# HGRN2 mixer of a 16-block network: work on keys, log decays and the first two levels moved between the weight slabs of its projections

## The reference

```python
q, f, i, g = jnp.split(h @ w_in, ...)                 # four projections, 1024 columns each
log_f = jnp.logaddexp(jnp.log(lb), jnp.log1p(-lb) + jax.nn.log_sigmoid(f))
k = -jnp.expm1(log_f)                                 # = (1 - lb) * sigmoid(-f)
q = jax.nn.silu(q);  v = i
# per head (8 heads of 128), cum = cumsum(log_f) over the tokens:
# o[t] = sum over s <= t of (q[t] * exp(cum[t] - cum[s]) . k[s]) v[s]
o = _rms(o, out_gain) * jax.nn.silu(g)
return o @ w_out
```

## Time and profile before

| | us |
|---|---|
| median of 3 runs | 2720.44 (2717.47 to 2721.78) |
| profiled execution: its own time | 2737.34 |
| profiled execution: span of the trace | 2735.2 |
| PE / DVE / ACT busy in the span | 2615.1 / 1762.1 / 1313.4 |
| PE / DVE / ACT share of the chain that ended last | 91% / 3% / 2% |

### The profile page before, as it was taken

How to read it: one execution, slowest core, us unless ns; L and a number is a source line. 1 busy time by engine, 2 the same in 40 slices (tenths; PEclk the granted TensorE clock), 3 DMA queues, 4 the chain that set the end, 5 groups by cost and what they waited for, 6 DMA issues and landing times.

```text
span 2735.2 us, 60697 instructions
## 1 busy us (share of the span) xinstructions
PE 2615.1 (96%) x23300; PEld 2545.4 (93%) x23300; DVE 1762.1 (64%) x2831; ACT 1313.4 (48%) x1947; POOL 74.4 (3%) x106
## 2 busy tenths in 40 slices
PE   7997999899999999999989999699999999999999
PEld 7996887899999999989989998689999999999999
DVE  5657565566756757766657656867667565555774
ACT  5544433355545546555445445345555454454552
POOL 0000442000000000000000000000000000000000
PEclk9999997899999999999999999899999999999999
DMA  5554200344555655445545645126655564452564
GB/s 197 188 185 130 94 3 33 109 154 153 190 188 179 202 194 183 158 139 184 192 146 184 206 155 165 43 98 199 206 173 196 179 183 123 135 141 95 170 209 144
DMA packets 114321, 424.24 MB, mean 155 GB/s; under 512 B 12433, under 2 KB 19044, under 8 KB 113796
## 3 DMA queue, kind: packets, MB, share of 16 engines
q1 hardware_dynamic: 105696, 408.99, 45.3%
q10 hardware_dynamic: 8484, 13.30, 2.3%
HBM read 421.12 MB, written 1.12 MB: 154 GB/s over the span
## 4 chain that ended last, share of the span: by engine, by line
PE 91%; DVE 3%; ACT 2%; issue 2%; DMA 0%; ACTq 0%; POOL 0%; DVEq 0%; SPq 0%; POOLq 0%
PE bank L462 21%; PE bank L464 21%; PE bank L463 21%; PE bank L396 5%; PE bank L397 4%; PE bank L398 4%; PE bank L2186 2%; PE bank L1605 1%; ACT hi L339 1%; PE bank L1580 1%; PE bank L443 1%; PE bank L444 1%; PE bank L445 1%; PE bank L1189 1%; PE bank L2114 1%
## 5 line engine op out<-in xcount | busy, mean ns | idle before, releaser
L347 DVE TENSOR_TENSOR lo<-raw,hi 128x1024 fp32r<-128x1024 f32 (+1 forms) x728 | 936.6, 1294 | 419.8 <-ACT hi L339 418.2
L339 ACT ACTIVATE hi<-raw 128x1024 fp32r<-128x1024 f32 (+1 forms) x728 | 787.4, 1106 | 361.3 <-PE bank L398 184.2
L462 PE MATMUL bank<-Hh,hi 128*128 128x256 f32 x3120 | 875.9, 281 | 18.4 <-DVE lo L347 18.1
L463 PE MATMUL bank<-Hl,hi 128*128 128x256 f32 x3120 | 874.3, 280 | 0.0
L464 PE MATMUL bank<-Hh,lo 128*128 128x256 f32 x3120 | 874.3, 280 | 0.0
L462 PEld LDWEIGHTS bank<-Hh,hi 128*128 128x128 f32 x3120 | 591.7, 190 | 21.4 <-DVE lo L347 20.4
L463 PEld LDWEIGHTS bank<-Hl,hi 128*128 128x128 f32 x3120 | 592.2, 190 | 0.0
L464 PEld LDWEIGHTS bank<-Hh,lo 128*128 128x128 f32 x3120 | 590.1, 189 | 0.0
L464 PE MATMUL bank<-Ah,lo 128*128 128x256 f32 x1408 | 394.0, 280 | 0.0
L463 PE MATMUL bank<-Al,hi 128*128 128x256 f32 x1408 | 393.9, 280 | 0.0
L462 PE MATMUL bank<-Ah,hi 128*128 128x256 f32 x1408 | 393.9, 280 | 0.0
(11 more groups left out here) (414 smaller groups left out, 4164.5 us busy)
## 6 DMA issues: line engine op xcount, KB each, us to landing
raw<-in_w SPq DMA_DIRECT2D x600, 512.0 KB, 3.4
raw<-in_w SPq DMA_DIRECT2D x128, 704.0 KB, 4.2
dB<-dil_bias ACTq DMA_DIRECT2D x16, 384.0 KB, 10.0
X<-in_x SPq DMA_DIRECT2D x2, 512.0 KB, 5.3
mem_x<-in_mem ACTq DMA_DIRECT2D x1, 1024.0 KB, 4.7
gWS<-in_ws ACTq DMA_DIRECT2D x1, 1024.0 KB
gBS<-in_bs ACTq DMA_DIRECT2D x1, 1024.0 KB
out_x<-X SPq DMA_DIRECT2D x4, 256.0 KB, 2.6
```

What stands on the lines that cost most here:

```text
L339: act.activation(k.hi[:, q, :w], k.raw[:, q, :w], ACT.Copy).then_inc(k.hi_ready, 1)
L347: dve.tensor_tensor(k.lo[:, q, :w], k.raw[:, q, :w], k.hi[:, q, :w].bitcast(F32), ALU.subtract).then_inc(k.lo_ready, 1)
L462: pe.matmul(out, wh, xh, start=first, stop=False)
L463: pe.matmul(out, wh, xl, start=False, stop=False)
```

## The change

1. Stage q: the split of the next slab stands ahead of the Silu on ScalarE (`split_first=True`).
2. The affine step with lb goes into ScalarE's Ln as its scale and bias, one Ln a head (8 of 128x256), and `K` is scaled by ScalarE in 8 copies. Both stand between the splits that belong to stage i. VectorE's 16 instructions of L1354 and L1358 are gone.
3. The 16 scans stand between the i slabs on VectorE (four after each of i2 to i5), subtract 0 after i6.
4. Stage g: Silu of G is taken once over the whole tile after the levels' exponentials, followed by a load of the table for Sqrt. TensorE's transposes stand behind g1, the products of level 0 behind g2 and of level 1 behind g6; both levels use banks 4 to 7. VectorE does multiply 0 behind g0, subtract 1 behind g1, take 0 behind g3 and g4, multiply 1 behind g5 and subtract 2 behind g6; the level loop after the stage starts with subtract 3 and multiply 2.

Stages i and g are written out slab by slab instead of a loop on ScalarE and VectorE, stage g on TensorE too. No product or transfer is added or taken away.

```diff
-    def act_stage(self, act, st, follow=None, between=None):
...
         def body(i, ahead):
             for q in range(RING):
-                if follow:
+                if follow and not split_first:
                     follow(i, q)
                 self.act_hi(act, st.base + RING * i + q + RING, q, ahead, st.base // RING + i + 1)
+                if follow and split_first:
+                    follow(i, q)
         run(act, st, body, between)
...
-        for x in "fig":
+        for x in "fi":
             sh.pe_stage_h(pe, sh.stage[f"hgrn_{x}"])
...
             for b in range(count // 4):
-                bank = 4 * (n % 2) + b
-                if n >= 2:
+                if n == 0:
+                    k.act_done.wait(pe, f"h.vt{b}")
+                elif n == 1:
+                    k.dve_done.wait(pe, f"h.take0.{b}")
+                elif n == 2:
+                    pe.wait_ge(k.banks_freed, RING + g + NC)
+                else:
                     k.dve_done.wait(pe, f"h.take{n - 2}.{b}")
...
-                    ins = pe.matmul(k.bank[bank][:, j * P:(j + 1) * P], left(4 * b + j), right(4 * b + j),
+                    ins = pe.matmul(self.gram_bank(n, b)[:, j * P:(j + 1) * P], left(4 * b + j), right(4 * b + j),
                                     start=True, stop=True)
                 k.pe_done.done(ins, f"h.gram{n}.{b}")
             n += 1
 
...
-        for lv in self.LEVELS:
+        def level():
             a = self.LV[n % 3]
             k.dve_done.wait(pe, f"h.lv{n}")
             half = lambda u: a[:, u // 2, (u % 2) * P:(u % 2 + 1) * P]
             gram(n, half, half, 2 * H)
+
+        def turn_values():
+            pe.wait_ge(k.banks_freed, RING + g)
+            pe.wait_ge(k.rstd_ready, sh.norm_n["pe"])
+            for b in range(4):
+                for j in range(4):
+                    c, half = 2 * b + j // 2, j % 2
+                    ins = pe.transpose(k.bank[4 + b][:, j * P:(j + 1) * P], self.V[:, c, half * P:(half + 1) * P], k.ident)
+                k.pe_done.done(ins, f"h.vt{b}")
+
+        for j in range(NC):
+            sh.pe_slab(pe, g + j, k.bank[j % RING], lambda kc: (k.Hh[:, kc, :], k.Hl[:, kc, :]), spare=RING)
+            if j == 1:
+                turn_values()
+            if j in (2, 6):
+                level()
+        for lv in self.LEVELS[2:]:
+            level()
...
-        project("q", self.Q)
-        project("f")
-
+        def log_decay(h):
+            s = self.LV[1][:, h, :]
+            d(act.activation(s, s, ACT.Ln, bias=C[:, 6, h:h + 1], scale=C[:, 7, h:h + 1]), f"h.lnf{h}")
+
+        def scale_key(h):
+            s = self.K[:, h, :]
+            d(act.activation(s, s, ACT.Copy, scale=C[:, 7, h:h + 1]), f"h.k{h}")
+
+        def split(x, j):
+            s = sh.stage[f"hgrn_{x}"].base + j
+            sh.act_hi(act, s + RING, s % RING, 8, s // RING + 1)
+
+        sh.act_stage(act, st, silu, split_first=True)
+        sh.act_stage(act, sh.stage["hgrn_f"])
         act.wait_ge(k.banks_freed, RING + sh.stage["hgrn_f"].base + NC)
         d(act.activation(self.LV[1][:], self.CUM[:], ACT.Sigmoid), "h.sig")
-        d(act.activation(self.K[:], self.CUM[:], ACT.Sigmoid, scale=-1.0), "h.nsig")
-        project("i")
-        k.dve_done.wait(act, "h.f7")
-        d(act.activation(self.LV[1][:], self.LV[1][:], ACT.Ln), "h.lnf")
+        for j in range(NC):
+            split("i", j)
+            if j == 0:
+                d(act.activation(self.K[:], self.CUM[:], ACT.Sigmoid, scale=-1.0), "h.nsig")
+                k.act_done.wait(act, "h.nsig")
+                k.dve_done.wait(act, "h.olb")
+            if 1 <= j <= 4:
+                for h in (2 * j - 2, 2 * j - 1):
+                    log_decay(h)
+            if 5 <= j <= 6:
+                for h in range(4 * j - 20, 4 * j - 16):
+                    scale_key(h)
         decays(0)
-        project("g", self.G)
-        for b in range(4):
-            k.pe_done.wait(act, f"h.vt{b}")
-            dst = self.VT[:, :, 2 * b * P:(2 * b + 2) * P].rearrange("p h (c j) -> p c h j", c=2)
-            d(act.activation(dst, k.bank[4 + b][:].rearrange("p (c h j) -> p c h j", c=2, h=2), ACT.Copy), f"h.vt{b}")
-        for n in range(1, len(self.LEVELS)):
+        for j in range(NC):
+            split("g", j)
+            if j == 1:
+                for b in range(4):
+                    k.pe_done.wait(act, f"h.vt{b}")
+                    dst = self.VT[:, :, 2 * b * P:(2 * b + 2) * P].rearrange("p h (c j) -> p c h j", c=2)
+                    d(act.activation(dst, k.bank[4 + b][:].rearrange("p (c h j) -> p c h j", c=2, h=2), ACT.Copy), f"h.vt{b}")
+            if j == 3:
+                decays(1)
+        for n in range(2, len(self.LEVELS)):
             decays(n)
         n = len(self.LEVELS) + 1
         a = self.LV[n % 3]
         k.dve_done.wait(act, f"h.d{n}")
         d(act.activation(a[:, :, P:], self.CUM[:, :, P:], ACT.Exp), f"h.er{n}")
         d(act.activation(a[:, :, :P], a[:, :, :P], ACT.Exp, scale=-1.0), f"h.el{n}")
+        act.wait_ge(k.banks_freed, RING + sh.stage["hgrn_g"].base + NC)
+        d(act.activation(self.G[:], self.G[:], ACT.Silu), "h.gate")
+        act.preload_act_table(ACT.Sqrt)
...
-        def take(n, name):
-            for b in range(4):
+        def take(n, name, quarters=range(4)):
+            for b in quarters:
                 k.pe_done.wait(dve, f"h.gram{n}.{b}")
-                ps = k.bank[4 * (n % 2) + b][:].rearrange("p (u t) -> p u t", u=4)
+                ps = self.gram_bank(n, b)[:].rearrange("p (u t) -> p u t", u=4)
...
-        k.act_done.wait(dve, "h.sig")
-        for h in range(H):
-            s = self.LV[1][:, h, :]
-            k.dve_done.done(dve.tensor_scalar(s, s, C[:, 7, h:h + 1], C[:, 6, h:h + 1], ALU.mult, ALU.add), f"h.f{h}")
-        k.act_done.wait(dve, "h.nsig")
-        for h in range(H):
-            s = self.K[:, h, :]
-            k.dve_done.done(dve.tensor_scalar(s, s, C[:, 7, h:h + 1], None, ALU.mult), f"h.k{h}")
-        project("i", self.V)
-        k.act_done.wait(dve, "h.lnf")
-        for h in range(H):
+
+        def slab(x, dst, j):
+            s = sh.stage[f"hgrn_{x}"].base + j
+            dve.wait_ge(k.slab_used, s + 1)
+            dve.tensor_tensor(dst[:, j, :], k.bank[s % RING][:, :T], k.R[:], ALU.mult).then_inc(k.banks_freed, 1)
+            sh.dve_lo(dve, s + RING, s % RING, 8)
+
+        def add_up(h):
+            k.act_done.wait(dve, f"h.lnf{h}")
             for half in range(2):
                 sl = slice(half * P, (half + 1) * P)
                 k.dve_done.done(dve.tensor_tensor_scan(self.CUM[:, h, sl], k.ones, self.LV[1][:, h, sl], 0.0,
                                                        ALU.mult, ALU.add), f"h.cum{h}.{half}")
-        k.dve_done.wait(dve, f"h.cum{H - 1}.1")
-        subtract(0, L[0])
-        project("g", self.G)
-        dve.wait_ge(k.proj_act, NC)
+
+        for j in range(NC):
+            slab("i", self.V, j)
+            if j == 2:
+                k.act_done.wait(dve, "h.nsig")
+            if 2 <= j <= 5:
+                add_up(2 * j - 4)
+                add_up(2 * j - 3)
+            if j == 6:
+                k.dve_done.wait(dve, f"h.cum{H - 1}.1")
+                subtract(0, L[0])
+        for j in range(NC):
+            slab("g", self.G, j)
+            if j == 0:
+                dve.wait_ge(k.proj_act, NC)
+                k.act_done.wait(dve, f"h.k{H - 1}")
+                multiply(0, L[0])
+            if j == 1:
+                subtract(1, L[1])
+            if j == 3:
+                take(0, f"pair{L[0]}", range(2))
+            if j == 4:
+                take(0, f"pair{L[0]}", range(2, 4))
+            if j == 5:
+                multiply(1, L[1])
+            if j == 6:
+                subtract(2, L[2])
...
         for n, lv in enumerate(L):
+            if n < 2:
+                continue
             if n + 1 < len(L):
...
-        dve.wait_ge(k.proj_act, 2 * NC)
+        k.act_done.wait(dve, "h.gate")
```

More of the change, by code:

```diff
@@ L411, in keys_lo, with act_stage @@
                                  ALU.mult, ALU.subtract).then_inc(k.kv_lo, 1)
-    def act_stage(self, act, st, follow=None, between=None):
+    def act_stage(self, act, st, follow=None, between=None, split_first=False):
         k = self.k
@@ L1160, in __init__, with gram_bank @@
         self.LEVELS = [6, 5, 4, 3, 2, 1, 0]
+    def gram_bank(self, n, b):
+        return self.k.bank[b + 4 * (n % 2 if n else 1)]
     def pe(self, pe):
@@ L1164, in pe @@
         sh.pe_first_stage(pe, sh.stage["hgrn_q"])
-        for x in "fig":
+        for x in "fi":
             sh.pe_stage_h(pe, sh.stage[f"hgrn_{x}"])
-        for b in range(4):
[L1168 to L1176, removed]
+        n, g = 0, sh.stage["hgrn_g"].base
         def gram(label, left, right, count):
@@ L1243, in act, with silu @@
         d(act.activation(C[:, 2:4, :], C[:, 0:2, :], ACT.Exp), "h.lbe")
[L1244 to L1251, removed]
```

(9 more changed lines are left out.)

## The result

The changed kernel took 2695.97 us, median of 20 runs (2679.2 to 2713.94), against 2714.84 us of the kernel before in 20 runs (2703.29 to 2731.49). The ratio of runs is 0.991, 95% interval 0.9891 to 0.9929: faster by 19 to 30 us (the medians themselves differ by 18.9). I had forecast 2699 us, a gain of 21.6.

What follows compares the result with a forecast made beforehand. The prediction took the mixer to be bound in some stages by the VectorE and ScalarE chain around TensorE, and by VectorE in the levels. Gains of 6.9 + 0.4 + 14.4 = 21.7 us gave 2699 us, range 2690 to 2710.

Steps and rivals of the forecast that it cites:

- Part 1: Stages q and f: with the split first, no slab from q4 to f7 is late; gain 6.9 us (4 to 7).
- Part 2: Stage i: the added ScalarE and VectorE work hides behind TensorE's 8 slabs; gain 0.4 us, or a loss of 0 to 3.
- the ring: Rival, stages i and g: scans and activations make a `lo` late in some six slabs, 9 us lost, 2708 us; chance 0.06.
- One sign: End of stage i: i7's move comes about 7 us earlier if the forecast is right.
- Part 3: Stage g up to subtract 3: TensorE's queue sets the time, 38.1 us instead of 52.5; gain 14.4 us (13 to 17).
- The other sign of this part: Stage g: 33 to 36 us from i7's move to g7's if the forecast is right.
- Part 4: Tail: Silu of G with two table loads, 4.5 us, fits in ScalarE's 10.36 us idle; nothing gained or lost.
- Sum: Whole kernel: the terms add to a gain of 21.7 us, scaled 21.6, from 2720.4 to 2698.8 us.
- The pace: Rival, blocks downstream: matmuls shift between 277 and 282 ns; slower gives 2707 us, chance 0.16, faster 2691, chance 0.05.
- My sign of being wrong: Block behind the mixer: matmuls at 282 ns instead of 277 would show the forecast wrong.
- The clock: Rival, stages g and o: three waits could bring TensorE to 1.2 GHz, 38 us lost, 2737 us; chance 0.04.
- The rule on the clock: Short idle spells between matmul groups can swing TensorE's clock and repeatedly cost throughput; by it 2737 us would be likely.

Runs made afterwards that it cites:

- both_mends: Changed kernel with ScalarE's stage q written out slab by slab and level 1's products behind g7; ratio 0.9909 to the kernel before, mixer 164.6 us.
- levels_behind_g: Changed kernel with the work of levels 0 and 1 and subtract 2 put back behind stage g; ratio 0.9948 to the kernel before, mixer 173.9 us.
- gate_only: Kernel before with only the Silu of G taken once behind the levels; ratio 0.9961 to the kernel before, mixer 180.2 us.
- the second pair of profiles: Kernel before and changed kernel, each unchanged, profiled a second time; mixers 188.5 and 170.1 us.
- warm_only: Changed kernel with only 22 and 20 unused matmuls added in TensorE's two gaps behind the levels; ratio 0.9922 to the kernel before, mixer 166.1 us.
- q_first_only: Kernel before with only the split put ahead of the Silu in stage q; ratio 0.998 to the kernel before, mixer 182.8 us.

## Why the prediction was right, and where its reading was not

- **Part 1, 6.9 us.** Measured 6.0 and 6.2. The step said a second table load "included once" makes none late. The changed order has a load at the head of each of the loop's two turns and another ahead of the Silu in each, four in all, as the rows of ScalarE show. The one ahead of the first split cost the 0.53 us before q4 (both_mends, where it is gone: f7 0.6 earlier); the rest of the 0.9 is not traced.
- **Part 2, 0.4 us.** Right: no wait of TensorE in stage i, the ring held with 1.36 us of scans behind each of four slabs. One sign failed: i7's move came 2.5 us earlier (71.0 against 73.5), not 7, since VectorE did subtract 0 first; TensorE itself was through i7 on time: two slabs before the transposes at 1668.44 is 1663.0, 21.4 us after f7's move.
- **Part 3, 14.4 us.** From f7 to subtract 3: 74.77 before, 59.63 after, 15.1 gained, against 0.4 + 14.4. Of this an estimated 0.7 us is the pace (191 slow steps of 4.5 ns in stages i and g before, 26 after); the second pair of profiles gives 14.7. The waits were 0.71 and 2.09 (0.4 and 2.1), the clock cost gram 1 1.6 us (0.8 taken), the slow pace less than taken. The size is right, what I wrote of its source is not: "The DVE work no longer there ... is the 12.04 us ... contained in the 14.4". levels_behind_g shows that those 12 us were traded for 12 us of TensorE in the same stage. The parts are the Silu chain of g (8.6, gate_only), the two levels (nothing beyond the pace), and a remainder of some 6 us by subtraction, in which the affine step has 1.2 to 1.5. I put the remainder down to the scans and subtract 0 out of the gap before g4; no run has them alone, so that is argued and not shown. That the sum came out within 1 us is in part luck, as 12 us were booked to a source that gave none. The other sign of this part failed as well: from i7's move to g7's were 31.7 us, not 33 to 36, because i7's move was late. From TensorE's end of i7 it is 35.9.
- **Part 4, nothing.** For the gate itself right: ScalarE had 7.18 us left. But the last stretch took 1.6 to 2.7 us more than before (43.3 and 44.2, 41.5 and 41.7). My sum held nothing for the clock there. warm_only shows that the clock moves this stretch. The gate alone doesn't account for it: 42.1 us with only the gate moved (gate_only), 41.5, 41.7 and 43.0 without (before, q_first_only). What sets the clock's course in each kernel stays open.
- **Sum.** 6.9 + 0.4 + 14.4 = 21.7; the mixer gave 19.4 and 18.4 (188.5 - 170.1), the runs 19 to 30. Terms missed: 0.9 in part 1, about 2 in the tail. The time itself was met within 3 us, on a base that lay lower too: 20 runs gave 2714.84 where three had given 2720.44.
- **The rivals.** The pace was real and larger than a single block, and fell on both kernels (five and six slow blocks before, five and three in the changed one): it widens the spread of runs, and nothing shows it to belong to the change. My sign of being wrong, 282 ns in the block behind, came in the first profile of the changed kernel and not in the second. My argument against this rival, three runs within 4.3 us, failed on 20 runs that spread over 28. The clock cost less than 2 us in stage g (window at 0.83; 0.95 over the 36 us of the stage); the ring never starved. The rule on the clock that I had weighed, from the Trainium skill's page "TensorE: Matmul & The Clock Gate" (section "A second HAM failure mode: psum-queue depth-cycling"), held for the last stretch, which the clock moved between 41.5 and 46.4 us (39.2 with TensorE kept busy), not for stage g.

## What to carry to other kernels

Work moved from a VectorE-bound stretch into a TensorE-bound one is paid again if it brings its matmuls with it: count both engines over the two stretches, and let only the part move whose products fit behind the stretch. Where an engine waits for a function between two steps of a weight ring, put the ring's step first, and read the order for table loads at a loop's head. And measure a local change by marks inside the profile, from one fixed instruction to another: the rest of a long kernel can shift by more than the change.

## What the runs showed of the hardware that I had not expected

- TensorE ran gapless stretches of the same matmuls at one of two paces, 2.72 or 2.83 us a slab of 24 (4%), different from one execution of the same code to the next, at a granted clock of 1.00. It turned 28 times of 28 at the norm's product near a block's start, and 21 times back soon after. What decides on that second turn is open; it wasn't tried.
- A serial stretch with short matmul bursts varied by 5 us over twelve profiles (41.5 to 46.4 us, granted clock 0.89 to 0.76), and 42 matmuls of no use took 3.0 to 5.9 us out of it (clock 0.96 and 0.98).
